# Two-layer trunk of a hybrid model: a PSUM bank for each kind of unit in the convolution stage, halves of a transposition in two units, half of a weight slab handed back early

## The reference

```python
for li in range(2):
    shift, scale, gate = split(silu(c) @ mod_w[li] + mod_b[li], 3)      # modulation; another for the context
    hx = rms_norm(x, norm_w[li]) * (1.0 + scale) + shift
    out_x, out_c = layer(hx, hc, ...)
    x = x + gate * out_x
# layer 0
q, k, v, ga, z, xbc, dt = split(h @ w_in)
xbc = silu(depthwise_conv(xbc, conv_w, conv_b))       # 5 taps along the tokens
xs, bm, cm = split(xbc)
y = bidir_ssd(xs, softplus(dt + dt_bias), a, bm, cm, d_skip, ...)
y = rms_norm(y * silu(z), ssm_norm)
out = concatenate([window_attention(q, k, v, ...) * silu(ga), y]) @ w_out
# layer 1: out = (rms_norm(diff_attend(q, k, v)) * silu(g)) @ w_out
```

## Time and profile before

| | us |
|---|---|
| median of 3 runs | 1154.6 (1154.49 to 1154.73) |
| profiled execution: own time | 1153.43 |
| its span | 1151.5 |
| TensorE busy, matmuls | 1105.1 (96%) |
| TensorE busy, weight loads (beside the matmuls) | 593.2 (52%) |
| VectorE busy | 593.3 (52%) |
| ScalarE busy | 362.1 (31%) |
| GpSimd busy | 176.5 (15%) |

### The profile page before, as it was taken

One profiled execution on the slowest core, in us unless ns is written; L12 is line 12 of the kernel. 1 busy time (PEld: TensorE's weight loads), 2 busy tenths in 40 slices (PEclk: granted clock), 3 DMA queues, 4 the chain that ended last, 5 costly groups with the idle time before them and its releaser, 6 DMA issues.

```text
span 1151.5 us, 11913 instructions
## 1 busy us (share of the span) xinstructions
PE 1105.1 (96%) x4259; PEld 593.2 (52%) x4259; DVE 593.3 (52%) x1235; ACT 362.1 (31%) x838; POOL 176.5 (15%) x168
## 2 busy tenths in 40 slices
PE   5999999899999999999999999999999999999988
PEld 1765555455554444555544444444455555556654
DVE  0456566576746376666410216511346654446776
ACT  1522112244422345444300112112234434334440
POOL 0301000098632200000000003300011210000000
PEclk9899999999999999999999999999999999999999
DMA  9914240457653101001003040222021030200001
GB/s 351 332 3 147 77 147 1 146 194 246 214 197 129 55 1 56 1 1 55 1 0 128 0 159 1 73 73 73 1 73 46 28 109 1 74 1 1 1 1 73
DMA packets 47345, 94.16 MB, mean 82 GB/s; under 512 B 2886, under 2 KB 4711, under 8 KB 47287
## 3 DMA queue, kind: packets, MB, share of 16 engines
q1 hardware_dynamic: 43701, 84.56, 21.0%
q10 hardware_dynamic: 3330, 8.67, 2.0%
q0 software_dynamic: 256, 0.18, 0.4%
HBM read 91.17 MB, written 2.23 MB: 81 GB/s over the span
## 4 chain that ended last, share of the span: by engine, by line
PE 90%; DVE 4%; SPq 2%; DMA 1%; ACT 1%; issue 1%; POOL 0%; DVEq 0%; ACTq 0%; POOLq 0%
PE ps L741 48%; PE ps L1004 10%; PE ps L932 7%; PE ps L1040 4%; PE ps L1062 4%; PE ps L904 3%; PE ps L951 2%; PE ps L916 2%; PE ps L983 2%; PE ps L1052 2%; PE ps L973 2%; PE ps L758 2%; DVE pool_mem L1199 1%; DMA xs_all<-in_x_dram 1%; PE ps L783 1%
## 5 line engine op out<-in xcount | busy, mean ns | idle before, releaser
L741 PE MATMUL ps<-ring,hT 128*128 128x512 f32 x736 | 320.5, 593 | 1.0 <-DVE hT L1183 1.0
L741 PEld LDWEIGHTS ps<-ring,hT 128*128 128x128 f32 x736 | 138.0, 190 | 165.4 <-issue 164.2
L741 PE MATMUL ps<-hT,ring 128*128 128x512 f32 (+1 forms) x512 | 172.2, 495 | 7.9 <-DVE pool_mem L1199 7.9
L741 PEld LDWEIGHTS ps<-hT,ring 128*128 128x128 f32 x512 | 98.6, 195 | 75.1 <-issue 67.6
L1821 POOL TENSOR_SCALAR stat<-stat 128x8 f32<-128x8 f32 (+3 forms) x52 | 20.4, 392 | 752.9 <-DVE stat L1379 237.5
L932 PE MATMUL ps<-ring,hT 128*128 128x512 f32 x192 | 88.9, 594 | 0.8 <-DVE pool_mem L1434 0.8
L1411 DVE TENSOR_REDUCE stat<-ps 128x1 f32<-128x768 f32 x64 | 60.9, 952 | 52.4 <-PE ps L1040 52.2
L1004 PE MATMUL ps<-ring,hT 128*128 128x512 f32 x192 | 85.7, 593 | 1.6 <-DMA ring<-in_ev_w_out_dram 1.6
L1478 DVE TENSOR_TENSOR pool_mem<-ps,pool_mem 128x512 f32<-128x512 f32 x36 | 24.8, 688 | 92.1 <-PE ps L1004 87.0
L1822 POOL TENSOR_TENSOR stat<-stat 128x8 f32<-128x8 f32 (+3 forms) x52 | 66.1, 1271 | 4.3
L1199 DVE SCALAR_TENSOR_TENSOR pool_mem<-ps,halftap,pool_mem 128x254 f32<-128x254 f32 (+3 forms) x96 | 59.1, 616 | 3.4
(11 more groups left out here) (202 smaller groups left out, 1439.2 us busy)
## 6 DMA issues: line engine op xcount, KB each, us to landing
ring<-in_mod_w_dram SPq DMA_DIRECT2D x10, 2048.0 KB, 8.0
ring<-in_od_w_in_dram SPq DMA_DIRECT2D x8, 2048.0 KB, 8.0
ring<-in_ev_w_in_dram SPq DMA_DIRECT2D x7, 2048.0 KB, 9.0
pool_mem<-la_rows_dram SPq DMA_DIRECT2D x24, 512.0 KB, 6.6
ring<-in_ev_w_out_dram SPq DMA_DIRECT2D x4, 1536.0 KB, 6.5
ring<-in_od_w_out_dram SPq DMA_DIRECT2D x2, 2048.0 KB, 8.0
ring<-in_mod_w_dram ACTq DMA_DIRECT2D x1, 2048.0 KB, 9.1
pool_mem<-in_mod_w_dram SPq DMA_DIRECT2D x1, 2048.0 KB, 20.4
```

Source lines behind the costliest of these rows:

```text
L741: mm = pe.matmul(bank[:, 0:width], lhs_of(k), rhs_of(k), start=(k == 0), stop=(k == count - 1))
```

## The change

1. In the convolution stage the bank no longer goes round: the 256-token product has index 0, the 512-token product index 1, everything between index 2. The stage of three banks ends with the last `xbc` instead of the last `diag`. `unit_banks` also takes a unit's bank when its first part starts, and holds it until the last, so that another unit inside it gets the other bank.
2. The single units of the convolution move between the two products of a block or right behind the second, `xtr` behind them.
3. The sums of the first four modulation parts (`modpick`) are matmuls with the operands exchanged: four of 128 x 2 a part, straight into columns of bank 6. The rows, their copies, the 16 transposes are gone.
4. SyncE issues tiles 0 and 1 ahead of the kvdt slab.
5. `ytr` of a tile: the first half before the last part of the next z (or output) unit, the second half inside the unit after that.
6. The first output slab (k 0 to 5 of the first half) is free when the third part of that half's last unit is done, and the second slab of the second half is loaded there (`HALF_READ`).
7. Of layer 1's fills, step 31 takes one in place of two, and the last stands behind the attention.

```diff
+HALF_READ = ("opart", 0, T_ORDER[-1], O_PARTS // 2 - 1)
...
-        st += [("xbc", f, 1), ("xbc", f, 0)]
-        if n >= 1 and conv_order[n - 1] not in (10, 11):
-            st.append(("xtr", conv_order[n - 1]))
+        st.append(("xbc", f, 1))
         if n == 1:
             st += [("dt", 2)] + [("eld", m) for m in range(4)]
...
+        if n - 1 in early:
+            st.append(("modsum",) + early[n - 1])
+        elif 5 <= n < 5 + NT:
+            st.append(("diag", n - 5))
+        st.append(("xbc", f, 0))
         if n in early:
             st.append(("mod",) + early[n])
-        if n - 1 in early:
-            st.append(("modsum",) + early[n - 1])
+        if n - 1 in early and 5 <= n < 5 + NT:
+            st.append(("diag", n - 5))
+        if n >= 1 and conv_order[n - 1] not in (10, 11):
+            st.append(("xtr", conv_order[n - 1]))
...
         if late:
-            parts[1].append(late.pop(0))
-            parts[3] += late
-            late = []
+            for j, stage in late.pop(0):
+                parts[j].insert(0, stage)
         if z[2] == 1:
             parts[3].append(("ysq", z[1]))
-            late = [("ynorm", z[1]), ("ytr", z[1], 0), ("ytr", z[1], 1)]
+            late = late or [[]]
+            late[0] += [(1, ("ynorm", z[1])), (3, ("ytr", z[1], 0))]
+            late.append([(1, ("ytr", z[1], 1))])
...
-        now = [fill.pop(0) for _ in range(1 + (n in (1, 2, 3, 9, 31)))]
+        now = [fill.pop(0) for _ in range(1 + (n in (1, 2, 3, 9)))]
...
+THREE_BANKS = range(UNIT[("kvdt", 0)], max(UNIT[s] for s in UNITS if s[0] == "xbc") + 1)
+def unit_banks():
+    bank, turn = [None] * len(UNITS), [None] * len(UNITS)
+    last, turns, held = [-2, -1, -3], [0, 0, 0], set()
+    for n, s in enumerate(STAGES):
...
+        if bank[m] is None:
+            if m in THREE_BANKS and u[0] != "kvdt":
+                bank[m] = {"xbc": 1 - u[-1]}.get(u[0], 2)
+            else:
+                bank[m] = min((b for b in range(3 if m in THREE_BANKS else 2) if b not in held), key=lambda b: last[b])
...
+            last[bank[m]] = n
+            held.add(bank[m])
+        if s == u:
+            held.remove(bank[m])
...
             for part in range(1, 4):
                 load_slab(SLAB_NO[("mod", 0, part)])
+            for t in range(2):
+                load_tile(t)
             load_slab(SLAB_NO[("kvdt",)])
...
+                if stage == HALF_READ:
+                    sp.wait_ge(half_read, 1)
+                    load_slab(HALF_SLAB)
...
+                elif kind == "modpick":
+                    wait_done(pe, ("mod", 0) + a)
+                    for j in range(4):
+                        col = 2 * (4 * a[0] + j)
+                        mm = pe.matmul(ps[:, 6, col:col + 2], mod_part0[:, a[0] % 2, j * P:(j + 1) * P], pick,
+                                       start=(col == 0), stop=True, skip_group_check=True)
+                    mm.then_inc(pick_ready, 1)
```

More of the change, by code:

```diff
@@ L190, in stages_layer0 @@
             if late:
-                parts[1].append(late.pop(0))
-                parts[-1] += late
-                late = []
+                for j, stage in late.pop(0):
+                    parts[j].insert(0, stage)
             pieces += parts
@@ L286 @@
                "k1", "v1", "q1", "g1", "hq", "hk", "pv1", "otr", "out1a", "out1b", "out1")
-UNITS = [s for s in STAGES if s[0] in UNIT_STAGES]
+UNITS = [s for s in STAGES if s[0] in UNIT_STAGES and s != ("modcol", 0)]
 UNIT = {s: n for n, s in enumerate(UNITS)}
 BANKS = (0, 1, 7)
[L290 to L298, removed]
+THREE_BANKS = range(UNIT[("kvdt", 0)], max(UNIT[s] for s in UNITS if s[0] == "xbc") + 1)
[3 more added lines that the diff above has]
+    for n, s in enumerate(STAGES):
+        u = {"zpart": ("z",), "opart": ("out0",)}.get(s[0], (s[0],)) + (s[1:3] if s[0] in ("zpart", "opart") else s[1:])
+        if u not in UNIT:
+            continue
+        m = UNIT[u]
+        if bank[m] is None:
[3 more added lines that the diff above has]
+                bank[m] = min((b for b in range(3 if m in THREE_BANKS else 2) if b not in held), key=lambda b: last[b])
+            turn[m] = turns[bank[m]]
+            turns[bank[m]] += 1
+            last[bank[m]] = n
+            held.add(bank[m])
+        if s == u:
+            held.remove(bank[m])
+    return bank, turn
+UNIT_BANK, UNIT_TURN = unit_banks()
 def slabs_of(stage):
@@ L343 @@
     LANDED.append(_landed[_p])
+HALF_SLAB = SLAB_NO[("out0", 1, 1)]
+assert PLACE[HALF_SLAB] == PLACE[SLAB_NO[("out0", 0, 0)]]
 def ordinal(kinds):
@@ L601, in wait_done @@
             eng.wait_ge(unit_done[UNIT_BANK[n]], UNIT_TURN[n] + 1)
-        def wait_done_upto(eng, stage):
-            n = UNIT[stage]
-            for m in range(n - (2 if n in THREE_BANKS else 1), n + 1):
-                eng.wait_ge(unit_done[UNIT_BANK[m]], UNIT_TURN[m] + 1)
         def bank_of(stage):
@@ L790, in _ @@
                 elif kind == "modcol":
-                    if a[0] == 0:
-                        wait_done_upto(pe, ("modsum", 0, 3))
-                        bank = begin(stage)
-                        for j in range(2 * KD):
-                            mm = pe.transpose(bank[:, 2 * j:2 * j + 2], mod_rows0[:, j * P:(j + 1) * P],
-                                              ident[0:2, 0:2])
-                        mm.then_inc(unit_ready, 1)
-                    else:
+                    if a[0] == 1:
                         pe.wait_ge(mod_rows, 16)
@@ L1208, in _ @@
                     dve.wait_ge(conv_tanh, n + 1)
-                    wait_done_upto(dve, ("xbc", f, 0))
+                    for part in (1, 0):
+                        wait_done(dve, ("xbc", f, part))
                     src = conv[:, ((at("xbc", f, 1) // 2)) % 3, :]
@@ L1227, in _ @@
                         V.tensor_copy(edges[:, P:3 * P], edges_f32).then_inc(edges_ready, 1)
-                        wait_done_upto(dve, ("kvdt", NT - 1))
+                        for t in range(NT):
+                            wait_done(dve, ("kvdt", t))
                         raw4 = dt_raw.rearrange("p (t d h) -> p d t h", t=NT, d=2)
@@ L1602, in _ @@
                     n = at(*stage) - 1
-                    wait_done_upto(act, ("xbc", f, 0))
+                    for part in (1, 0):
+                        wait_done(act, ("xbc", f, part))
                     if n >= 2:
```

51 lines of the change are left out of this document (30 added, 21 removed).

## The result

The changed kernel takes 1135.28 us (median of 4 runs, 1133.28 to 1136.97) against 1154.66: ratio 0.983, 95% interval 0.981 to 0.985. Repeated later it took 1135.25 us (4 runs, 1135.21 to 1135.90) against 1154.03. So it gained 19 us where 22.1 were forecast. The profiled execution took 1136.97 us (span 1135.1) where 1131.3 were forecast; it is the slowest of the four, and the one profiled before the change (1153.43) was the fastest there.

What follows compares the result with a forecast made beforehand. TensorE, busy 1105.1 of 1151.5 us, was taken as the bound. Gains of 2.0 + 11.5 + 6.7 + 1.6 + 0.3 = 22.1 us gave 1131.3 profiled, 1132.5 median; 8-in-10 range 1129 to 1137.

Steps and rivals of the forecast that it cites:

- Start, 2.0: Kernel start: tiles loaded ahead of the kvdt slab let squaring begin at 27.95 instead of 29.92; gain 2.0 us, picks nothing.
- a rival on the convolution: Start and convolution: low clock stays, elsewhere; both convolution stretches come back, 3.5 us, 1136.0; chance 0.10.
- Convolution, 13.1 gross: Convolution waits for VectorE's taps removed: 7.9 us idle, 3.5 low clock, 1.7 drain and refill; 13.1 us before new waits.
- The term for drain and refill, 1.7: Convolution: each removed tap wait also saves 0.33 us of drain and refill around it, 1.7 us in all.
- New waits, 1.6: Convolution: 0.8 us for ScalarE's last kvdt copy, and 0.4 in each of two blocks for the long unit's bank.
- The margin of 0.2 us: Convolution: 4.5 us of work covers the long unit's bank wait of 4.3; rival that it is missing: 1136.5, chance 0.12.
- Turning, 7.4 gross: Turning the gated output in the attention: five turns at 1.33 us and a sixth at 0.7; 7.4 us, net 6.7.
- the difference 2.23 less 0.90: Turning: both halves lasted 2.23 us, eight records without a wait 0.90, so 1.33 us gained per turn.
- Half slab, 1.6: Last output slab issued after the third of six parts, 5.2 us earlier; its wait of 1.6 us ends.
- tail, 0.3: Last block: one output unit moves behind the last value products; between -0.5 and +1.0, taken as a gain of 0.3 us.
- The start gained no more than forecast: Rival at the start: the 5.1 us half-clock stretch after 32.90 goes, 2.6 us more, 1129.9; chance 0.10.
- The taps set no pace: Rival in the convolution: fixed banks make the taps the pace, 11 second products waiting 2.5 us each, 1160; chance 0.02.

Runs made afterwards that it cites:

- old sums: Changed kernel with the modulation sums of before instead of the picks, last kvdt unit in bank 1: 1136.41 us; with wide matmuls as well, 1134.45 us.
- old loads: Changed kernel with the kvdt slab ahead of all token tiles again, picks kept: 1136.57 us; with wide matmuls as well, 1137.21 us.
- wide matmuls: Changed kernel plus 20 matmuls of 128 moving columns that nobody reads, placed where TensorE idled at the start: 1132.52 us, ratio to before 0.982.
- the order alone: Changed kernel with its new order of convolution units, but that stage's banks going round again: 1139.06 us (one run), convolution stretch 148.70.
- the banks alone: Changed kernel with its fixed banks, but the convolution's units in the old order: 1140.52 us (one run), convolution stretch 150.04.
- A mended wait elsewhere: Wide-matmul version with last kvdt unit in bank 1 and a bank counted as used at its unit's end: 1130.89 us, ratio to before 0.980.
- the old turning: Changed kernel with both halves of a turn behind the z or output unit again: 1138.68 us (one run), attention stretch 168.42.

## Why the prediction was right, and where not

The time lay in the range, 2.8 us above the forecast. The direction held, and the waits went that it had named; in the start and in the convolution it had the cause only in part. Of its signs, the one for being wrong at the start (first transposition later than 31.5) came true in the profiled execution, 33.66, and not in the repeat, 30.85; the first gate product came 9.9 us earlier than 220.3 in the one and 11.8 in the other, not 13.5. The missing microseconds, by its own steps:

- **Start, 2.0.** The squaring follows ScalarE's copy of part 3 as forecast, and the transpositions begin at 30.85 in the typical execution against 30.9. But the forecast put the 2.0 down to the loads alone. In the kernel before, the row copies kept ScalarE until 0.21 us before the squaring, so early loads without the picks would have given that much at most: with old sums it squared at 29.76, with old loads at 30.18, with both changes at 27.86. Two more premises failed in the profiled execution. Modulation part 3 and its copy did not stay where the earlier trace rows have them: 1.7 us. And the picks were taken at nothing, because only the last group follows the copy of part 3. In the queue the group before it stands behind part 3 too; the two took 3.58 us at the low clock (the bound of 1.8 each held), and VectorE's scaling of the tile stands behind the columns: 1.1 us. Both came with the low clock, and both were gone in the repeat: +0.8 in the one, -2.05 in the other. And of those 2.05, 0.7 are given back: the stretch from the first transposition to the end of the kvdt stage (without the new wait) takes 31.98 us in the repeat and 31.29 before; it begins earlier, so more of it lies in the low stretch. The rule that I had put beside a rival, that the gate samples free-running beside the kernel (the Trainium skill, TensorE: Matmul & The Clock Gate, Part 1), fits the two executions of one program: TensorE's groups begin within 0.06 us of each other from 14.5 to 20 us, and from 19.9 to 21.1 us the granted clock is 0.50 in the repeat and 0.99 in the other. It belonged in the start's term, not only in a rival on the convolution. The wide matmuls show that TensorE's own work has a part in it as well.
- **Convolution, 13.1 gross.** The forecast gave the gain to the banks; the order alone does more than the banks alone (7.4 and 6.1 us). Idle time 7.9 became 0.5; the low stretches, 3.5, went, as no run with fixed banks shows any from 65 us to the first gate product. The term for drain and refill, 1.7, was mis-sized: 144.93 less 0.48 of waits is 144.45, and 156.11 less 7.9 and 3.5 is 144.71, so 0.3 is left for it. A mended wait elsewhere did bring 0.15 to 0.23 beyond its idle time. So either waits of this stage had less, or the added changes between kinds of unit cost it again; the run with the old order (150.04 less 5.4 of waits, 144.6) does not decide it.
- **New waits, 1.6.** The one for ScalarE's copy was 0.70 (0.8), those on the long unit's bank 0.24 twice (0.4 twice). The margin of 0.2 us in the other blocks held.
- **Turning, 7.4 gross.** Right place, wrong size: five times 1.03, not 1.33, and 0.5 for the sixth, together 5.6. Against it 0.55 for the output unit, as forecast (0.6), and 0.35 more for the probabilities, which was not. 4.7 net, measured 4.67. The step that failed is the difference 2.23 less 0.90: it takes the halves to cost the same when each stands alone between products, and what came back with the old turning is the idle time alone.
- **Half slab, 1.6, and tail, 0.3.** 1.82 and 0.16 to 0.22.
- **Rivals.** The low clock did not return in the convolution. The start gained no more than forecast; with wide matmuls it would (transposes at 30.79 and 2.4 GHz behind them, the stretch to the convolution 30.60 us for 32.68 in the repeat, so 2.1 us of the 2.6 priced; 1132.5 in all). The taps set no pace.

For the typical execution the account closes: 0.5 at the start, 1.1 in the convolution, 0.5 between gate and score (185.30 for 184.84), 2.0 in the turning and 0.1 at the end are missing, 0.2 is over, 4.0; forecast 1131.3, measured 1135.26.

## What to carry to other kernels

As these runs have it, price a removed wait at its idle time, and book the drain and refill around it only if the new order has fewer breaks than the old. Where TensorE works in bursts, its clock in one profile is a draw: profile twice before building on a time there, and consider filling the gaps with matmuls that nobody reads. Here 20 of them kept the clock at 2.4 GHz up to 31 us and gave 2.8 us, though not always behind that: with the old loads, where TensorE idled 3.8 us for a tile, and with the old sums a low stretch followed. A bank per kind of unit and an order that spaces the units remove the same waits; try each alone to know which rule to keep.

## What the runs showed of the chip

- One program, two executions, two clock patterns: part 3 of the modulation 3.64 or 1.92 us. With wide matmuls in the gaps the granted clock from 17 to 31 us was 1.00 in all five profiled executions; without, 0.65 to 0.88 in all nine.
- A wait of 1.65 us was followed by the 1.2 GHz level in one version and not in another that reached it 0.8 us later; during a wait of 3.39 us it set in, after one of 2.11 us in the run with the old order it did not.
- A pick group, eight matmul records with 2 moving columns, takes 1.05 us at 2.4 GHz and 1.8 at 1.2 GHz, 0.13 and 0.22 us a record. The wide matmuls, twenty records with 128 moving columns, take 2.48 us at 2.4 GHz, 0.12 a record. So here a record with 2 moving columns cost no less than one with 128.
